# Seven block products in place of eight for gate and up in the last block of an fp32 trunk layer

## The reference

```
h    = RMSNorm(x)
proj = h @ w_in                       # queries, keys, values, indexer, gates of both mixers
o_a  = sliding-window attention with sinks,  o_b = top-256 sparse attention
x    = x + (sigmoid(gate_a) * (o_a @ w_branch_a) + sigmoid(gate_b) * (o_b @ w_branch_b)) @ w_out
h2   = RMSNorm(x)
ff   = silu(h2 @ w_ffn_gate) * (h2 @ w_ffn_up)      # 1024 -> 2816
x    = x + ff @ w_ffn_down
out  = RMSNorm(x)
```

## Time and profile before

| | |
|---|---|
| median of 3 runs | 3200.07 us (3198.18 to 3200.74) |
| span of the profiled execution | 3196.7 us |
| PE busy | 3156.0 us, 99% |
| DVE, ACT, POOL busy | 1814.8, 1420.8, 2036.0 us |
| moved by DMA | 392.59 MB, 123 GB/s over the span |

### The profile page before, as it was taken

How to read it: one execution, slowest core, us unless ns; L and a number is a source line. 1 busy time by engine, 2 the same in 40 slices (tenths; PEclk the granted TensorE clock), 3 DMA queues, 4 the chain that set the end, 5 groups by cost and what they waited for, 6 DMA issues and landing times.

```text
span 3196.7 us, 44024 instructions
## 1 busy us (share of the span) xinstructions
PE 3156.0 (99%) x15678; PEld 2655.0 (83%) x15678; DVE 1814.8 (57%) x3706; ACT 1420.8 (44%) x2589; POOL 2036.0 (64%) x2201
## 2 busy tenths in 40 slices
PE   9999999999999999999999999999999999999998
PEld 7888888878878888888888888988888799888887
DVE  3335546537565545557666666967868689521111
ACT  3324435435473534337354534837655378320001
POOL 5666766665556666764666676366767922666676
PEclk9999999999999999999999999999999999999999
DMA  5765455355615333331533334163333500533332
GB/s 152 198 167 172 119 154 157 103 157 163 209 35 182 102 112 107 108 125 57 201 104 116 103 102 138 28 238 103 98 109 112 171 23 17 180 91 99 95 103 99
DMA packets 464201, 392.59 MB, mean 123 GB/s; under 512 B 29264, under 2 KB 394064, under 8 KB 463344
## 3 DMA queue, kind: packets, MB, share of 16 engines
q1 hardware_dynamic: 442544, 345.56, 36.0%
q10 hardware_dynamic: 21440, 44.22, 3.7%
HBM read 323.76 MB, written 62.81 MB: 121 GB/s over the span
## 4 chain that ended last, share of the span: by engine, by line
PE 92%; POOL 2%; ACT 2%; DVE 2%; issue 1%; DMA 1%; SPq 0%; POOLq 0%; ACTq 0%; DVEq 0%
PE BANK L1049 22%; PE BANK L1051 21%; PE BANK L1050 21%; PE LP L1049 4%; PE LP L1051 4%; PE LP L1050 4%; PE BANK L1330 3%; PE BANK L1355 2%; PE LP L1166 2%; PE LP L1165 2%; PE LP L1310 2%; PE LP L1311 2%; PE BANK L1357 2%; POOL WLO L986 1%; POOL WHI L984 1%
## 5 line engine op out<-in xcount | busy, mean ns | idle before, releaser
L986 POOL TENSOR_TENSOR WLO<-WRAW,WHI 128x512 fp32r<-128x512 f32 x912 | 1213.3, 1330 | 76.0
L984 POOL TENSOR_SCALAR WHI<-WRAW 128x512 fp32r<-128x512 f32 x912 | 639.6, 701 | 776.1 <-PE BANK L1051 622.1
L1049 PE MATMUL BANK<-H2hi,WHI 128*128 128x512 f32 x1376 | 538.7, 392 | 1.1 <-POOL WLO L986 1.1
L1050 PE MATMUL BANK<-H2lo,WHI 128*128 128x512 f32 x1376 | 535.9, 389 | 0.0
L1051 PE MATMUL BANK<-H2hi,WLO 128*128 128x512 f32 x1376 | 535.8, 389 | 0.0
L1049 PE MATMUL BANK<-HThi,WHI 128*128 128x512 f32 (+1 forms) x1024 | 405.1, 396 | 0.8 <-DVE QS L2044 0.5
L1050 PE MATMUL BANK<-HTlo,WHI 128*128 128x512 f32 (+1 forms) x1024 | 399.4, 390 | 0.0
L1051 PE MATMUL BANK<-HThi,WLO 128*128 128x512 f32 (+1 forms) x1024 | 399.3, 390 | 0.0
L1751 ACT ACTIVATE MASK<-SCD,THR 128x896 bf16<-128x896 f32 (+5 forms) x186 | 281.9, 1516 | 191.8 <-DVE THR L2104 164.6
L1051 PEld LDWEIGHTS BANK<-H2hi,WLO 128*128 128x128 f32 x1376 | 258.3, 188 | 54.4
L1049 PEld LDWEIGHTS BANK<-H2hi,WHI 128*128 128x128 f32 x1376 | 258.6, 188 | 53.3 <-issue 1.3
(11 more groups left out here) (314 smaller groups left out, 6457.6 us busy)
## 6 DMA issues: line engine op xcount, KB each, us to landing
WRAW<-in_w_in SPq DMA_DIRECT2D x124, 512.0 KB, 4.2
WRAW<-in_w_ffn_gate SPq DMA_DIRECT2D x88, 512.0 KB, 3.8
WRAW<-in_w_ffn_up SPq DMA_DIRECT2D x88, 512.0 KB, 3.8
WRAW<-in_w_ffn_down SPq DMA_DIRECT2D x88, 512.0 KB, 3.5
qsp<-QS SPq DMA_DIRECT2D x32, 512.0 KB, 5.8
WRAW<-in_w_out SPq DMA_DIRECT2D x32, 512.0 KB, 4.6
gates<-GS ACTq DMA_DIRECT2D x62, 256.0 KB, 2.2
GL<-gates ACTq DMA_DIRECT2D x48, 256.0 KB, 4.5
```

Of the source, the lines that this page charges most:

```text
L984: nc.gpsimd.tensor_scalar(hi, raw, 1.0, 1.0, ALU.mult, ALU.mult).then_inc(w_hi, 1)
L986: nc.gpsimd.tensor_tensor(lo, raw, hi.bitcast(f32), ALU.subtract).then_inc(w_split, 1)
L1049: nc.tensor.matmul(dst, whi, mhi, start=first, stop=False)
L1050: nc.tensor.matmul(dst, whi, mlo, start=False, stop=False)
```

## The change

Block 3's gate and up products from tile 2 on (`by_seven`), 20 tiles, leave the list of jobs. Contraction and rows are cut in halves (4 of 8 weight tiles, 256 of 512 rows), gate and up weights are seen as the two columns of one 2 x 2 block matrix, and the 2 x 2 block product is formed of seven block products in place of eight, with four operands on the weight side that are sums of gate and up halves, and four on the activation side that are differences of quarters of h2. A product is 4 contraction tiles times 3, 12 matmuls of 256 columns.

- The weight sums are formed once, in block 0's projections. At job i from 9 to 28 SP loads the gate and the up tile of q = i - 9 to WS[q % 3], DVE adds four times (`sum_weights`), and at jobs 11 to 30 SP stores the 1 MB of the result to DRAM (`wsd`).
- At block 3's feed-forward SP loads for each tile the 1 MB of sums, half of the up tile and the gate tile (`load_units`). Each product's weights, a unit, are rounded by ACT to a ring of eight (`high_unit`, six ahead), and their low part is made by POOL, for units 2 and 5 of each seven by DVE.
- DVE forms the activation differences before and between tiles 0 and 1 (`first_differences`, `last_differences`), ACT rounds them.
- Partial results that two outputs share are copied by ACT from PSUM to C1U and C5 and added by DVE; the shared first product has places of its own in LP0.
- The wait for the last norm's gains moves with SP's loads of block 3.

The diff, cut to its core:

```
+    SEVEN = FT - DIRECT
+    HK, HR = KT // 2, ROWS // 2
+    RING, LEAD = 8, 6
+    ON_VECTOR = (2, 5)
     C = Count(known)
     n, made = C.n, C.made
...
+        GRAW = [at(f"GRAW{i}", [P, KT, P], f32, (rO, r1 + 12288)[i]) for i in range(2)]
+        URAW = [at(f"URAW{i}", [P, HK, P], f32, rO + 4096 + 2048 * i) for i in range(2)]
+        SRAW = [at(f"SRAW{i}", [P, 2 * KT, P], f32, (rX + 32768, r1 + 4096)[i]) for i in range(2)]
+        UHI = [at(f"UHI{i}", [P, HK, P], f32r, rX + 4096 * i) for i in range(RING)]
+        ULO = [at(f"ULO{i}", [P, HK, P], f32r, rX + 4096 * i + 2048) for i in range(RING)]
+        HF = [at(f"HF{i}", [P, HK, HR], f32, rX + 16384 + 4096 * i) for i in range(4)]
+        THI = [at(f"THI{i}", [P, HK, HR], f32r, rT + 4096 * i) for i in range(4)]
+        TLO = [at(f"TLO{i}", [P, HK, HR], f32r, rK + 4096 * i) for i in range(4)]
+        C1U = [at(f"C1U{i}", [P, 2, HR], f32, zone + 2048 * i) for i in range(2)]
+        C5 = at("C5", [P, HR], f32, zone + 4096)
...
+        def unit_raw(u):
+
+            q, c = u // 7, u % 7
+            if c in (0, 6):
+                return gate_raw[q % 2], GRAW[q % 2][:, c // 6 * HK:(c // 6 + 1) * HK, :]
+            if c == 5:
+                return up_raw[q % 2], URAW[q % 2][:, :, :]
+            part = {1: 3, 2: 2, 3: 0, 4: 1}[c]
+            return sums_raw[q % 2], SRAW[q % 2][:, part * HK:(part + 1) * HK, :]
+
+        def unit_low(u):
+
+            return unit_low_dve if u % 7 in ON_VECTOR else unit_low_pool
+
...
             return [((kind, b, m), weights(w_in, range(KT), COL[kind] + m * P, width)) for m in range(tiles)]
@@ -303,6 +349,8 @@
         def ffn_jobs(b, part):
             jobs = []
             for i in part:
+                if by_seven(b, i):
+                    continue
...
+            def load_weights_to_add(q):
+
+                w, i = WS[q % 3], q + DIRECT
+                if q >= 3:
+                    sp.wait_ge(wsum_out[q % 3], n(wsum_out[q % 3], ("sums", q - 3)))
...
+                made(wsum_in[q % 3], ("sums", q), 32)
+                sp.dma_start(w[:, 0:KT, :], weights(io["w_ffn_gate"][0], range(KT), i * P)).then_inc(wsum_in[q % 3], 16)
+                sp.dma_start(w[:, KT:2 * KT, :], weights(io["w_ffn_up"][0], range(KT), i * P)).then_inc(wsum_in[q % 3], 16)
+
+            def store_sums_of_weights(q):
+
+                sp.wait_ge(wsum_ready, n(wsum_ready, ("sums", q)))
+                made(wsum_out[q % 3], ("sums", q), 16)
+                sp.dma_start(io["wsd"][q], WS[q % 3][:, :, :].rearrange("p k c -> p (k c)")).then_inc(wsum_out[q % 3], 16)
+
+            loaded = [0]
+
+            def load_units(stop):
...
+                    i, s = q + DIRECT, q % 2
+                    if q == 0:
+                        sp.wait_ge(bank_full, n(bank_full, ("br", NB - 1, KT - 1, 1)))
+                        for v in range(SEVEN - 3, SEVEN):
+                            sp.wait_ge(wsum_out[v % 3], n(wsum_out[v % 3], ("sums", v)))
+                    if q == 1:
+                        sp.wait_ge(bank_full, n(bank_full, ("x2t", NB - 1, 1, KT // 2 - 1)))
+                    if q >= 2:
+                        for c in (1, 2, 3, 4):
+                            u = 7 * (q - 2) + c
+                            sp.wait_ge(unit_low(u), n(unit_low(u), ("unit", u)))
+                    made(sums_raw[s], ("unit", q), 16)
+                    sp.dma_start(SRAW[s][:, :, :].rearrange("p k c -> p (k c)"), io["wsd"][q]).then_inc(sums_raw[s], 16)
+                    if q >= 2:
+                        u = 7 * (q - 2) + 5
+                        sp.wait_ge(unit_low(u), n(unit_low(u), ("unit", u)))
+                    made(up_raw[s], ("unit", q), 16)
+                    sp.dma_start(URAW[s][:, :, :], weights(io["w_ffn_up"][0], range(HK, KT), i * P)).then_inc(up_raw[s], 16)
+                    if q >= 2:
+                        u = 7 * (q - 2) + 6
+                        sp.wait_ge(unit_low(u), n(unit_low(u), ("unit", u)))
+                    made(gate_raw[s], ("unit", q), 16)
+                    sp.dma_start(GRAW[s][:, :, :], weights(io["w_ffn_gate"][0], range(KT), i * P)).then_inc(gate_raw[s], 16)
+                    if i == PARTS[-1][2]:
+                        load_last_norm(NB - 1)
+                loaded[0] = max(loaded[0], stop)
...
                 first_attention(i - PROJ + len(projections(NB - 1)))
+                if key[0] == "fd" and key[2] == NB - 1 and key[3:] == (0, 0):
+                    load_units(key[1] + SLOTS - DIRECT + 1)
                 if i >= 2:
                     sp.wait_ge(w_split, 2 * (i - 1))
                 if width > P:
@@ -807,6 +912,12 @@
                 sp.dma_start(raw, src).then_inc(w_in_sem[i % 2], 16)
...
+                if 0 <= i - 9 < SEVEN:
+                    load_weights_to_add(i - 9)
+                if key == ("fu", NB - 1, 0):
+                    load_units(1)
                 b = key[2] if key[0] == "fd" else key[1]
                 LAST = PARTS[-1][0]
                 if key == ("br", b, 1, 1):
@@ -843,9 +954,7 @@
...
+            def low_unit(u):
+
+                if u >= 7 * SEVEN or u % 7 in ON_VECTOR:
+                    return
+                pool.wait_ge(unit_hi, n(unit_hi, ("unit", u)))
+                nc.gpsimd.tensor_tensor(ULO[u % RING][:, :, :], unit_raw(u)[1], UHI[u % RING][:, :, :].bitcast(f32),
+                                        ALU.subtract).then_inc(unit_low_pool, made(unit_low_pool, ("unit", u)))
+
+            def low_units(part, first_job):
+
+                pairs = [i - DIRECT for i in part if by_seven(NB - 1, i)]
+                if pairs[0] == 0:
+                    for u in range(LEAD):
+                        low_unit(u)
+                for q in pairs:
+                    for c in range(7):
+                        low_unit(7 * q + c + LEAD)
+                        if (q, c) == (pairs[-2], 5):
+                            split(first_job)
+                        if (q, c) == (pairs[-1], 3):
+                            split(first_job + 1)
+
...
                     scale_late(key[1])
                 k, place = pair_place(key[1], key)
@@ -1028,7 +1163,7 @@
         def _(pe):
             rings = dict(bank=[(0,), (1,), (2,), (3,)], pair=[(0,), (1,), (2,), (3,)], values=[(0,)], trans=[(1,), (2,), (3,)],
                          low=[(4,), (5,), (6,), (7,)], logits=[(4, 5), (6, 7)], near_scores=[(4, 5)], near_turn=[(6,), (7,)],
-                         near_values=[(6,), (7,)], held=[(3,)])
+                         near_values=[(6,), (7,)], held=[(3,)], seven_gate=[(0,), (1,)], seven_up=[(2,), (3,)], seven_first=[(4,), (5,)])
             taken, owner = {kind: 0 for kind in rings}, {}
             job_no = [0]
 
...
+                def seven(i):
+
+                    q = i - DIRECT
+
+                    def product(c, dst, half, side, first, t=None):
+
+                        u = 7 * q + c
+                        if q == 0 and t is not None:
+                            pe.wait_ge(t_split, n(t_split, ("t", t)))
+                        pe.wait_ge(unit_low(u), n(unit_low(u), ("unit", u)))
+                        for s in range(HK):
+                            hi, lo = ((THI[t][:, s, :], TLO[t][:, s, :]) if t is not None else
+                                      (quarter(w, half, side)[:, s, :] for w in (H2hi, H2lo)))
+                            whi, wlo = UHI[u % RING][:, s, :], ULO[u % RING][:, s, :]
+                            nc.tensor.matmul(dst, whi, hi, start=first and s == 0, stop=False, skip_group_check=True)
+                            nc.tensor.matmul(dst, whi, lo, start=False, stop=False, skip_group_check=True)
+                            last = nc.tensor.matmul(dst, wlo, hi, start=False, stop=(s == HK - 1), skip_group_check=True)
+                        last.then_inc(product_done, made(product_done, ("product", u)))
+
+                    low, high = slice(0, HR), slice(HR, ROWS)
+                    both = take("seven_first", copied, ("copy", q, 2), ("fc", q))
+                    product(0, both[:, low], 0, 0, True)
+                    gate = take("seven_gate", silu_ready, (b, i), ("fg", b, i))
+                    product(1, gate[:, high], 0, 0, True, 0)
+                    up = take("seven_up", ff_split, (b, i), ("fu", b, i))
+                    product(2, up[:, low], 0, 0, True, 1)
+                    pe.wait_ge(copied, n(copied, ("copy", q, 0)))
+                    product(3, both[:, low], 0, 0, False, 2)
+                    pe.wait_ge(copied, n(copied, ("copy", q, 1)))
+                    product(4, gate[:, high], 1, 1, False)
+                    pe.wait_ge(corner_ready, n(corner_ready, ("corner", q)))
+                    product(5, up[:, low], 0, 0, False, 3)
+                    product(6, gate[:, low], 1, 0, True)
...
+                def high_unit(u):
+
+                    if u >= 7 * SEVEN:
+                        return
+                    landed, raw = unit_raw(u)
```

(85 more changed lines are left out.)

115 lines of the change are left out of this document (112 added, 3 removed).

## The result

The changed kernel takes 3306.2 us (median of 4 runs, 3305.81 to 3308.79), the kernel before 3199.4 in the same comparison; the ratio is 1.0337, 95% interval [1.0325, 1.0349]. It is slower, as forecast, but by 107 us and not by 50: outside the range of 3222 to 3293. The profiled spans are 3304.0 and 3196.7 us, 107.3 apart.

The account below looks back on a forecast made before the run. PE bounds the kernel, but DMA would bound block 0's projections. 3196.7 + 58.7 - 5 (weight sums) - 7.6 (products) + 4 (start) = 3246.8; with 3.4 outside the span, 3250 us; 80% range 3222 to 3293.

Parts of the forecast that it names:

- the signs: Block 0's projections: WRAW lands in over 10 us instead of 4.6, DMA slices at 9 tenths, PE at 6 to 7.
- The step that failed: Block 0's projections: DVE waits for a tile's loads and is one job late, PE has four banks, so nothing is added.
- Rival C: Block 0: transfers cost their full single price, or order on SP and DVE leaves DMA idle; 84 not 54, 3280; chance 0.10.
- the bytes' upper end: Block 0's projections: weight sums' transfers at prices of packets that travel alone, 218.6 us in all, 89 more.
- The bytes' term: Block 0's projections: 65.1 MB at 345 GB/s take 188.7 us in place of 130, 58.7 more.
- a lead of 5: Block 0: a WRAW can land some 5.8 us later before PE stands still, once; about 5 us off the loss.
- The seven products: Block 3's gate and up: 84 short matmuls a tile, 10.48 us, win 0.38 us a tile, 7.6 over 20 tiles.
- The bound for hidden waits: Block 3's gate and up: if the products' semaphore waits are hidden, 9.95 us a tile, 18 us won in all.
- the middle between bounds: Block 3: one 0.075 us wait per product, 10.48 us a tile, taken between 9.95 and 10.93.
- My mark for being wrong: Block 3: forecast 1.50 us for a product of 12 matmuls; wrong if under 1.43 or over 1.56.
- The start: Block 3's first tile of seven: DVE's differences and low halves come late, one stall of 0 to 9 us, taken as 4.
- rival B: Block 0's projections: PE's clock falls to its lower level in the gaps; held throughout, 105 us more, 3301; chance 0.08.

Follow-up runs that it names:

- the ring open: Two variants of the changed kernel: weight sums' loads and stores one job later, 3256.93 us; or DVE's additions left out, 3256.86 us.

## Why the prediction was right and wrong

**The sign, and the place.** Right: the weight sums lose far more in block 0 than the products win in block 3, DMA can't carry them, and PE waits for WRAW there. The bytes were right too: 65.1 MB forecast, and the trace has 65.19 from 55 to 308 us, though at a mean of 258 GB/s. Of the signs, WRAW landed in 7.1 us (median from 55 to 308 us), later than 4.6 but not over 10, as DMA stood idle in each turn of the ring.

**The step that failed** is the sentence that closes the weight sums' part: DVE waits in order for a tile's loads, DVE is a job late then, PE has four banks, "so that adds nothing". I followed that delay to PE's banks and stopped. I didn't follow it to SP, where the store waits for the same sums, ahead of the next store of queries, which frees the buffer that DVE's own next step needs. The ring costs 49 us (118.6 against 69.8 and 69.5 with it open), most of the miss of 56. The four banks did not cover DVE's delay either: PE waited 33.0 us for DVE's QS, and 15.1 with the ring open. The earlier trace rows could not show it, since nothing waited there before; the diff could: sums i-11 stand 7 jobs later in DVE's order, at i-4, and queries i-6 with two buffers free the same i-4, so there is no slack. Rival C names "the order on SP and DVE" in passing, without a mechanism, and prices it with the bytes' upper end; 3306 lies beyond it.

**The bytes' term** was 58.7 less a lead of 5. With the ring open it is 69.8. The rate was 327 GB/s (65.1 MB in 130 + 69.2 us), not 345. Whether a lead came off isn't shown: the WRAWs lag from job 13 on (3.2 us, then 7.7 at job 14), and PE's first long wait there, 8.2 us, is for DVE's QS and not for POOL. If the 5 us did come off, the rate was 65.1 / 204.2 = 319. So the rate was chosen 5 to 8% high, if it is the engines' (what else it may be stands with the runs above). The upper end of 89 us, by the price of a packet alone, was not reached: that price held for the loads and was too high for the stores. The Trainium skill ("DMA: Bandwidth & Descriptors", Specifications) has about 358 GB/s for HBM's share of a core. The trace of the kernel with 4 KB rows holds 365 for 100 us, near that figure and above it; with 512-byte loads the runs have 327 over the same 100 us and 347 in the stage from 120 to 180.

**The seven products** were forecast to win 0.38 us a tile, 7.6 in all; they win 0.80 a tile, 16.0. The pitch of 0.1185 was right to 0.0015. The 0.075 us for each product's wait was wrong: the earlier trace rows shows it once in a first gate that was just beginning, and in a steady stream a wait that is already met costs nothing. The bound for hidden waits (9.95, 18 us) was close (10.08, 16), and the middle between bounds was no evidence. My mark for being wrong, a product under 1.43 or over 1.56 us, does not catch it at 1.44, though it is not the 1.50 forecast either.

**The start** was forecast at 4 us, for DVE's unit 2 and for ACT's copy behind it. The first tile of seven is 3.2 us over the others, with PE's two waits, 1.10 and 1.29 us, at these two places. Two waits for POOL's WLO, 0.73 at 2964.92 and another of 0.69, come to 1.4: 4.6 in all. 16.0 - 4.6 = 11.4, and the feed-forward won 11.3. That the total is near 4 is in part luck: the WLO waits were not foreseen. The last section shows what POOL was slowed by there.

**PE's clock** (rival B) did fall, to 0.60 from 100 to 150 us, and I had listed that as a sign that I would be wrong. The kernel with PE kept busy shows that it was no cause.

**The sum by measured terms:** 3196.7 + 69.8 (bytes) + 48.8 (ring) - 16.0 (products) + 4.6 (start) = 3303.9; the profiled span is 3304.0. The ring's term is the difference of the two lags and not a measurement of its own, so the agreement checks only the feed-forward's terms.

## What to carry to other kernels

Where a change puts a wait into an in-order queue, walk from it all the way round (who fills that semaphore, what stands before it there, which buffer frees that, who stores the buffer) and add up the offsets; here a ring whose sum was zero cost a whole round trip a turn, and one iteration more on one link opened it. A stage that slows down while no engine, DMA included, is busier than before is a sign of such a ring rather than of bandwidth. Traffic that doesn't fit may not be needed: ask whether the data will be in SBUF later anyway, on an engine with time to spare.

## What the runs showed of the hardware

**DVE and POOL slow each other in SBUF.** Around the first tile of seven in the changed kernel (2963 to 2984 us), where DVE works on 1024-element operations out of SBUF, POOL's groups are (line, operation, count, busy and mean ns)

```profile
L1095 POOL TENSOR_TENSOR WLO<-WRAW,WHI 128x512 fp32r<-128x512 f32 x2 | 4.2, 2123 | 0.2
L1093 POOL TENSOR_SCALAR WHI<-WRAW 128x512 fp32r<-128x512 f32 x1 | 1.6, 1589 | 0.0
```

against 1285 ns and 0.62 us for the same shapes, and DVE's 512-element difference is at 1728 ns there:

```profile
L2794 DVE TENSOR_TENSOR ULO<-SRAW,UHI 128x512 fp32r<-128x512 f32 x2 | 3.5, 1728 | 0.5 <-ACT UHI L2149 0.5
```

It goes both ways: in the chain above, POOL is busy from 156.88 to 161.59 us, and DVE's additions of 512 elements beside it take up to 1.68 us; the last of the four, from 162.18 on with POOL idle, takes 0.70. And this is what lay behind the waits at the start: from 2953.45 to 2968.5, where POOL splits two jobs, each half takes it 3.8 us where it had 1.9. What I had in the earlier trace rows (791 and 1088 ns) lies between. Which of the two engines holds the other, and by what, the runs don't tell apart.

**Issuing a DMA isn't of constant cost.** In the timeline from 241 us on, with DMA's share at 1.01, the store of sums takes SP 3.47 us and the piece of the table 4.94, where they took 0.34 in the ring and about 0.5 before; SP's next instruction starts only after. It does not go by the DMA's own size: the store of 64 KB took 3.52.
